# Ten of the sixteen normed tiles of x transposed by DMA from ScalarE's queue instead of by TensorE, their squares written to PSUM

## The reference

```python
def _rmsnorm(x, gain):
    y = x32 * lax.rsqrt(jnp.mean(x32 * x32, axis=-1, keepdims=True) + NORM_EPS)
    return y * gain

xn = _rmsnorm(h, norm_g)                       # h: 16 meta rows, then x
proj = jnp.einsum("bld,de->ble", xn, w_in)     # all projections read xn
v_c, g_c, z_c, u_s, z_s, gl_c, gl_s = _split_columns(proj)
y_c = _conformer_conv(v_c, g_c, z_c, ...)
y_s = _s5_scan(u_s, ...)
merged = gate_c * (y_c @ w_conv) + gate_s * (y_s @ w_ssm)
out = _rmsnorm(h + merged @ w_out, final_g)[:, N_META:, :]
```

## Time and profile before

| what | value |
|---|---|
| runs of the kernel | 1695.3, 1871.41 and 2025.17 us, median 1871.41 us |
| profiled execution | 1696.1 us |
| its span on the slowest core (core 7) | 1694.5 us |
| spans of the eight cores | 1686.1 to 1694.5 us, granted TensorE clock 0.995 to 0.998 |
| PE busy | 1649.5 us, 97% of the span |
| DVE, ACT, POOL busy | 728.1, 513.7, 60.5 us |

### The profile page before, as it was taken

How to read it: one execution, slowest core, us unless ns; L and a number is a source line. 1 busy time by engine, 2 the same in 40 slices (tenths; PEclk the granted TensorE clock), 3 DMA queues, 4 the chain that set the end, 5 groups by cost and what they waited for, 6 DMA issues and landing times.

```text
span 1694.5 us, 22937 instructions; the slowest of 8 cores (1686.1 to 1694.5 us)
## 1 busy us (share of the span) xinstructions
PE 1649.5 (97%) x8974; PEld 799.3 (47%) x8974; DVE 728.1 (43%) x1116; ACT 513.7 (30%) x739; POOL 60.5 (4%) x129
## 2 busy tenths in 40 slices
PE   5999999999999999999999999999999999999998
PEld 3544555555554444455554444444444444444443
DVE  4672788788830003375724311111111337543333
ACT  4753677777731110013321611111111000021111
POOL 1000000000000001000000000000000000000000
PEclk9999999999999999999999999999999999999999
DMA  9813122323257224992141303022221435454443
GB/s 227 227 63 50 47 67 58 81 57 78 54 113 137 50 38 55 116 113 48 27 92 31 57 13 63 1 38 38 38 38 38 139 116 182 162 184 149 149 150 124
DMA packets 33468, 148.58 MB, mean 88 GB/s; under 512 B 3969, under 2 KB 7169, under 8 KB 24193
## 3 DMA queue, kind: packets, MB, share of 16 engines
q0 software_dynamic: 13456, 58.20, 22.4%
q1 hardware_dynamic: 19906, 88.91, 15.1%
HBM read 178.03 MB, written 40.89 MB: 129 GB/s over the span
## 4 chain that ended last, share of the span: by engine, by line
PE 91%; ACT 4%; DMA 4%; issue 1%; DVE 1%; POOL 0%; DVEq 0%; ACTq 0%; SPq 0%; POOLq 0%
PE ps L257 89%; PE ps L260 2%; DMA wu<-wu 2%; ACT cs L229 1%; DMA dwb<-dw_b 1%; DMA xt<-x 1%; ACT L229 1%; ACT yc L229 0%; ACT wv L229 0%; ACT gst L229 0%; DVE xs L245 0%; ACT tt L229 0%; ACT xs L231 0%; DVE h L245 0%; POOL wu L263 0%
## 5 line engine op out<-in xcount | busy, mean ns | idle before, releaser
L257 PE MATMUL ps<-xm,wr 128*128 128x512 bf16 x1280 | 296.1, 379 | 1.6 <-ACT gst L229 1.6
L257 PE MATMUL ps<-wb,xm 128*128 128x512 bf16 x1024 | 226.6, 382 | 0.0
L257 PE MATMUL ps<-xm,zr 128*128 128x512 bf16 x1024 | 223.0, 379 | 0.0
L257 PE MATMUL ps<-wo,m 128*128 128x512 bf16 x1024 | 221.2, 379 | 0.0
L257 PEld LDWEIGHTS ps<-xm,wr 128*128 128x128 bf16 x1280 | 119.8, 98 | 129.5 <-issue 4.9
L257 PE MATMUL ps<-xm,gr 128*128 128x512 bf16 x768 | 169.7, 379 | 0.0
L257 PEld LDWEIGHTS ps<-wo,m 128*128 128x128 bf16 x1024 | 100.2, 98 | 120.8
L257 PEld LDWEIGHTS ps<-wb,xm 128*128 128x128 bf16 x1024 | 100.1, 99 | 120.2 <-issue 5.2
L257 PEld LDWEIGHTS ps<-xm,zr 128*128 128x128 bf16 x1024 | 99.7, 98 | 118.2
L231 ACT ACTIVATE jk<-h 128x2048 bf16<-128x2048 f32 (+1 forms) x19 | 31.2, 1641 | 324.8 <-DVE h L245 324.8
L257 PE MATMUL ps<-wu,xm 128*128 128x512 bf16 x512 | 116.8, 386 | 8.1 <-DMA wu<-wu 4.6
(11 more groups left out here) (168 smaller groups left out, 1722.5 us busy)
## 6 DMA issues: line engine op xcount, KB each, us to landing
xt<-x SPq DMA_DIRECT2D x16, 1024.0 KB, 8.5
x<-x SPq DMA_DIRECT2D x16, 1024.0 KB, 6.9
out<-h SPq DMA_DIRECT2D x15, 1024.0 KB, 4.7
wr<-wm POOLq DMA_DIRECT2D x20, 512.0 KB, 7.8
gscr<-gst SPq DMA_DIRECT2D x20, 512.0 KB, 7.5
gr<-gscr SPq DMA_DIRECT2D x20, 512.0 KB, 3.4
wob<-wo POOLq DMA_DIRECT2D x8, 1024.0 KB, 24.1
zr<-wm POOLq DMA_DIRECT2D x16, 512.0 KB, 6.1
```

The costliest lines, as they stand in the source:

```text
L257: return S.op("pe", lambda e: e.matmul(out_, lhsT, rhs, start=start, stop=stop), r, w, signal=signal)
```

## The change

The transposes of entries 7 to 16 are no longer done by PE. For each of these ten entries ACT issues one DMA that transposes the whole tile from `xs` into `xm`, with a completion semaphore of its own (four in turn). It stands one entry earlier in the order: in the step of A(i) it is T(i+3) where T(i+2) stood. With the 160 transposes on PE go the ten copies on DVE and the ten on ACT that brought them from PSUM to `xm`. The square of these ten entries writes its unread result to PSUM, over the banks 0 to 3 in one piece, instead of to `xs`; so that one access can reach over four banks, the PSUM is allocated as two tensors of four banks and not four of two.

```diff
+        pst = [es.enter_context(nc.psum_tensor(f"ps{i}", [128, 2048], F32)) for i in range(2)]
+        ps2 = [t[:, h * 1024:(h + 1) * 1024] for t in pst for h in range(2)]
...
+        DT0 = 7
...
-            act(xs, xt, AF.Square, accum=q, r=(bx,), w=(bs, STB[i]))
+            if i >= DT0:
+                act(pst[0][:, :], xt, AF.Square, accum=q, r=(bx,), w=tuple(PB[0:4]) + (STB[i],))
+            else:
+                act(xs, xt, AF.Square, accum=q, r=(bx,), w=(bs, STB[i]))
...
+        def trans_dma(i):
+            t = seq[i]
+            S.op("act", lambda e: e.dma_start_transpose(
+                out=XM.ap[:, t // 4, :, (t % 4) * 128:(t % 4 + 1) * 128], in_=XS[i % 2].ap),
+                 (XSb[i % 2],), (XMB[t],), src=XTR[i % 4])
...
-            if i + 2 < NSEQ:
+            if i + 2 < DT0:
                 order += [f"T{i + 2}"]
+            if DT0 <= i + 3 < NSEQ:
+                order += [f"T{i + 3}"]
...
-                trans(i)
+                if i >= DT0:
+                    trans_dma(i)
+                else:
+                    trans(i)
```

More of the change, by code:

```diff
@@ L220, in buf @@
                            self.hi if hi is None else self.lo + hi)
-        pst = [es.enter_context(nc.psum_tensor(f"ps{i}", [128, 1024], F32)) for i in range(4)]
-        ps2 = [t[:, :] for t in pst]
+        pst = [es.enter_context(nc.psum_tensor(f"ps{i}", [128, 2048], F32)) for i in range(2)]
+        ps2 = [t[:, h * 1024:(h + 1) * 1024] for t in pst for h in range(2)]
         ps = [ps2[j // 2][:, (j % 2) * 512:(j % 2 + 1) * 512] for j in range(8)]
@@ L411, in trans @@
                    pT.rearrange("p (k t) -> p k t", k=8), r=(PB[bk],), a=(XMB[t],))
+        XTR = [dsrc() for _ in range(4)]
+        def trans_dma(i):
[3 more added lines that the diff above has]
+                 (XSb[i % 2],), (XMB[t],), src=XTR[i % 4])
         def xmt(j, k):
```

## The result

| | before | after |
|---|---|---|
| median of the runs beside each other | 1783.36 us (four, 1693.94 to 2025.17) | 1735.95 us (four, 1733.58 to 1739.57) |
| profiled execution | 1696.1 us | 1738.26 us |
| spans of the eight cores | 1686.1 to 1694.5 us | 1714.8 to 1736.7 us |

In some executions the cores of one die run at a lower clock; these are left out of every ratio, and where too few were left for a ratio, the text gives the median span of the cores of undisturbed dies. Compared in this way the change is slower: 1.0245 times the time before, 95% interval 1.0223 to 1.0266, some 41 us. The forecast was 1694 us.

A forecast was written before the change was run, and what follows sets the result against it. PE, busy 1649.5 of 1694.5 us, bounds the kernel, with x loading setting the stage's pace until about 72 us. Waits lose 2.2 us up to A10, T12 to T16 save 4.5: net -2.3, 1694 us; range 1685 to 1720.

The forecast's parts named there:

- The issue on ACT, 0.53 us: Time each of the ten transpose issues holds ACT, taken from POOL's converting issue; also the lower bound, with 0.34 us.
- The upper bound of 7.8 us: Issue on ACT at most: ACT goes through the tile piece by piece for as long as a whole converting transfer.
- The landing of T7, 10.3 us: Transfer time for T7 to T9, which meet the x loads; 7.8 us for later ones, ends 3.4 and 18.8 us.
- The expected gap ahead of A7, 5.9 us: PE finishes A6 at 60.5 us and waits for T7, landing at 66.4; the pause may lower PE's clock.
- From A10 on pure gain: From A10 each transfer lands one entry early, so the five transposes T12 to T16 save PE 4.5 us.
- ACT's loop: Square, root, copy of A's result, issue, next square in ACT's queue: 5.5 us, against 7 to 10 us of PE per entry.
- The held ACT: Rival, chance 0.25: the issue holds ACT; 3 us an issue gives 1697 us, 7.8 us gives 1727 us.
- The slow transfer with two `xs` buffers: Rival, chance 0.15: entry i+2 waits until T(i) has read its buffer; 18.8 us a transfer gives 1718 us.
- the estimate was 1.5 us of transfer: Transfer time for a tile by the skill's 350 to 400 GB/s; supports the everything-hidden rival, 1687 us, chance 0.15.
- The transposes saved: 160 transposes removed from PE: 0.9 us for a tile, 9.0 us for ten.
- The square into PSUM: Square of entry 7 waits for banks 0 to 3 and delays the meta transposes: 0.8 us lost once; 2.0 us against 1.91.
- the second price: After a pause PE may run at its lower clock: 16 products took 5.30 us in place of 3.6.

The follow-up runs named there:

- wu_early: Changed kernel with POOL's last two pieces of `wu` called for earlier, behind the meta rows: 1.0168 times the kernel before; a core 1718.3 us.

## Why the prediction was wrong, step by step

**The issue on ACT, 0.53 us: the step that failed.** It was taken from POOL's issue of a converting copy, and measured 1.38 to 20.88 us on core 3, with a median of 4.25. The upper bound of 7.8 us was formed from the right picture, that ACT is held for as long as the transfer goes, but from a transfer of another kind, and as one price for all ten. What the runs show in its place is a length that is tied to the traffic: 2.5 us as a median without most of the x loads, 4.2 with them, 20.9 where T7's packets crawled.

**The landing of T7, 10.3 us: the second term that failed.** It took 27.9 us on core 3, and the gap ahead of A7 is the largest of the stage on seven of the eight cores. The row of 10.3 us came from the same stretch of full DMA engines, but the engines were full of large packets at 252 GB/s; with a transpose's packets among them, 2080 for a tile and some 250 bytes each, they were full at 66 GB/s (why is open, see the last section). The expected gap ahead of A7, 5.9 us, was there, with 23.38 us. T12, beside which an x load was just ending, landed in 4.3 us, nearer to the plain copy's 3.4 than to the 7.8 us that I took; T9 to T15 took 4.3 to 9.5 us, about what the sum had for them.

**What comes behind.** "From A10 on pure gain" failed with the first step: ACT's loop was long enough to make PE wait for `u` (11.8 us) and `ut` (5.4 us). My loop had only the transfers in it that PE waits for. It left out that the copies which empty PE's banks, and through the reciprocal DVE's table work, stand in the same queue.

**The rivals.** The held ACT was the right mechanism. Its working at 3 us (1697) and 7.8 us (1727) assumed that each issue is equally long and that PE loses only by late transfers; the runs lie beyond both. The slow transfer with two `xs` buffers did not become a loop: T7 and T8 were slow, and T16 at the end (13.6 us), but not the seven between them. By the rule of the Trainium skill, "VectorE: DVE Perf Modes", section "The three transpose paths", this rival had an estimated 20.9 us for a tile; T12's 4.3 us don't agree. By that of the Trainium skill, "Advanced Engine Details and Errata", section "X-Bar Transpose (TRN2)", the estimate was 1.5 us of transfer; T12's packets moved 215 to 219 GB/s while it was alone on the DMA engines, and 512 KB in its 4.3 us from issue to landing are 122 GB/s, so that this one isn't borne out either. That the issue costs little is also what the Trainium skill leads one to expect, "DMA: Bandwidth & Descriptors", section "Issuing engines are not separate DMA queues": it says that the choice of the issuing engine only saves time on the sequencer, which is usually small beside the transfer. Here it was 20.88 of 22.9 us; the measurement decides.

**What held.** The transposes saved 0.9 us each: the balance above closes with it. The square into PSUM delayed the meta entry's transposes by 1.08 us (expected 0.8), and takes 1.88 us where it took 1.91. PE's pauses had the second price that the prediction named, the lower clock, and paid it four times. The copies that went from ACT and DVE were worth nothing, as expected. Nothing outside the stage changed.

**Shares of the 33 us on a core.** ACT's in-order queue: 28 us go when the issue moves to SP, with T7 a little sooner. The x traffic: 21 go when most of it is cut. These overlap, since the traffic sets how long ACT is held.

## What to carry to other kernels

Price a DMA transpose at the queue that issues it, not only at its landing: the queue may stand for nearly the whole transfer, so issue it where nothing else that is needed waits in order, or behind the next piece of compute. Keep it out of stretches where the DMA engines are full: here one landed in 27.9 us in such a stretch and in 4.3 us behind it, and the loads beside it got late too. On an engine that is not the bottleneck, list what else passes through its queue (bank releases, another engine's inputs) before a wait there is called free.

## What the hardware showed that I had not expected

The issues on ACT were not all held: in the kernel after, the first, fifth and ninth (T7, T11, T15) took 1.48, 2.73 and 1.38 us on core 3 (T11 took 1.37 on core 0), and in the kernel with the cut x loads 1.45, 1.42 and 1.33. T7 was released at once although it took 27.9 us to land. Over the eight cores these three took 1.33 to 2.73 us, and the other seven 2.06 to 22.19. That they share one semaphore is not the reason: with entries 12 to 16 alone the first and fifth are T12 and T16, which use another of the four, and took 1.46 and 1.53 us on core 3. It looks as if room is given back every four transposes, but this is not shown: with the issue behind the next square the fifth took 1.34 to 2.56 us over the cores, and the third and fourth 1.8 to 2.4, and on SP's queue, which carries x loads as well, the pattern wasn't there (T7 took 7.28 us). The cause stays open; another number of semaphores or smaller transposes were not tried.

Open too is why x loads, a converting load and a transpose together fall to 66 GB/s. A transpose beside x loads is not slow in itself: while T9 on core 0 ran beside one x load, the engines were full (0.99) and moved 285 GB/s over 5 us. That POOL's load is needed isn't shown either. Without it the gap ahead of A7 is shorter as a rule, but on core 6 of that run (wu_early) an x load and the transposes alone moved 23 and 34 GB/s between 70 and 74 us, with the DMA engines nearly idle (shares of 0.06 and 0.15). And on core 1 of the kernel after, all three were under way from 62 to 68 us and moved 315, 234 and 137 GB/s in each 2 us. By what mechanism a transfer gets stuck is not known.
